# The output projection of the dilated layer, cut into chunks of 256 inputs and placed between the last four heads

## The reference

```
def second_block(x, c, ...):
    cond = silu(c)
    for i in range(2):
        mod = (cond @ ada_w[i] + ada_b[i]).reshape(B, 6, D)
        h = rms_norm(x, norm_mix[i]) * (1 + scale1) + shift1
        y = mla_mixer(h, ...) if i == 0 else dilated_mixer(h, ...)
        x = x + gate1 * y
        h = rms_norm(x, norm_mlp[i]) * (1 + scale2) + shift2
        x = x + gate2 * (square(relu(h @ mlp_w1[i])) @ mlp_w2[i])

def dilated_mixer(h, pos, w_in, g_q, g_k, rel_bias, w_o):
    # three groups of windows and dilations, 16 heads of 64; softmax over all of them
    ...
    return o.reshape(B, S, 1024) @ w_o
```

## Time and profile before

| | us |
|---|---|
| median of 3 runs | 1710.52 (1708.68 to 1711.46) |
| the profiled execution | 1711.83 |
| its span | 1709.9 |

### The profile page before, as it was taken

The page is one execution under the profiler, slowest core; times in us unless marked ns, Lnnn a source line. Parts: engine busy times, 40 slices in busy tenths (PEclk is TensorE's granted clock), DMA queues, the critical chain, the costliest instruction groups (busy, mean ns, idle before and its releaser), DMA issues.

```text
span 1709.9 us, 29065 instructions
## 1 busy us (share of the span) xinstructions
PE 1637.5 (96%) x12246; PEld 1544.7 (90%) x12246; DVE 1100.8 (64%) x1382; ACT 814.2 (48%) x1064; POOL 111.0 (6%) x99
## 2 busy tenths in 40 slices
PE   7999999999999999999888999989999999899998
PEld 6999989998999999999878899978999999889997
DVE  5768667775677668776685666667666555165554
ACT  5545443444545454444676544445444444254442
POOL 1040000000140000000020000001111110000000
PEclk9999999999999999999998999999999999599999
DMA  8765366666676456566432466666856454045552
GB/s 277 249 220 191 130 232 210 226 204 216 224 263 222 148 192 218 197 234 227 136 116 75 137 238 226 229 230 222 271 175 220 137 171 142 21 134 194 185 181 95
DMA packets 230242, 325.57 MB, mean 190 GB/s; under 512 B 7672, under 2 KB 199648, under 8 KB 229600
## 3 DMA queue, kind: packets, MB, share of 16 engines
q1 hardware_dynamic: 218696, 313.00, 54.5%
q10 hardware_dynamic: 11416, 10.71, 2.0%
HBM read 314.23 MB, written 9.45 MB: 189 GB/s over the span
## 4 chain that ended last, share of the span: by engine, by line
PE 75%; issue 9%; DVE 8%; ACT 4%; POOL 2%; DMA 1%; ACTq 0%; SPq 0%; DVEq 0%; POOLq 0%
PE bank L506 23%; PE bank L507 22%; PE bank L508 22%; PE bank L549 2%; DVE wlo L1496 2%; ACT whi L1044 2%; POOL rstd L983 2%; PE bank L570 1%; PE bank L874 1%; PE bank L702 1%; DVE ada_raw L1506 1%; PE bank L632 1%; DMA raw<-in_w_ffn_in 1%; PE bank L897 1%; DMA raw<-in_w_in 0%
## 5 line engine op out<-in xcount | busy, mean ns | idle before, releaser
L1496 DVE TENSOR_TENSOR wlo<-raw,whi 128x2048 fp32r<-128x2048 f32 (+1 forms) x241 | 550.5, 2287 | 282.2 <-ACT whi L1044 282.0
L1044 ACT ACTIVATE whi<-raw 128x2048 fp32r<-128x2048 f32 (+1 forms) x241 | 455.8, 1894 | 120.6 <-PE bank L508 96.9
L506 PE MATMUL bank<-hT_hi,whi 128*128 128x256 f32 x1728 | 495.6, 287 | 0.6 <-issue 0.3
L507 PE MATMUL bank<-hT_lo,whi 128*128 128x256 f32 x1728 | 490.3, 284 | 0.0
L508 PE MATMUL bank<-hT_hi,wlo 128*128 128x256 f32 x1728 | 490.1, 284 | 0.0
L506 PEld LDWEIGHTS bank<-hT_hi,whi 128*128 128x128 f32 x1728 | 332.6, 192 | 7.1 <-issue 5.5
L507 PEld LDWEIGHTS bank<-hT_lo,whi 128*128 128x128 f32 x1728 | 332.9, 193 | 1.2
L508 PEld LDWEIGHTS bank<-hT_hi,wlo 128*128 128x128 f32 x1728 | 332.8, 193 | 0.0
L506 PE MATMUL bank<-whi,hT_hi 128*128 128x256 f32 (+1 forms) x944 | 275.4, 292 | 4.1 <-DVE qn L1604 2.2
L507 PE MATMUL bank<-wlo,hT_hi 128*128 128x256 f32 (+1 forms) x944 | 270.4, 286 | 0.0
L508 PE MATMUL bank<-whi,hT_lo 128*128 128x256 f32 (+1 forms) x944 | 270.3, 286 | 0.0
(11 more groups left out here) (276 smaller groups left out, 1611.1 us busy)
## 6 DMA issues: line engine op xcount, KB each, us to landing
raw<-in_mlp_w SPq DMA_DIRECT2D x64, 1024.0 KB, 5.5
ada_raw<-in_ada_w SPq DMA_DIRECT2D x96, 512.0 KB, 6.2
raw<-in_w_in SPq DMA_DIRECT2D x44, 1024.0 KB, 5.4
raw<-in_w_ffn_in SPq DMA_DIRECT2D x44, 1024.0 KB, 5.3
raw<-in_dil_w_in SPq DMA_DIRECT2D x36, 1024.0 KB, 5.0
raw<-in_w_ffn_out SPq DMA_DIRECT2D x22, 1024.0 KB, 4.9
raw<-in_w_o SPq DMA_DIRECT2D x8, 1024.0 KB, 5.2
bias_near<-near SPq DMA_DIRECT2D x2, 3072.0 KB, 10.3
```

The lines of the kernel that those rows point to most:

```text
L506: pe.matmul(dst, lh, rh, start=start, stop=False)
L507: pe.matmul(dst, lh, rl, start=False, stop=False)
L1044: act.activation(view(whi[c % SPL], c), view(raw[c % RAW], c), ACT.Copy).then_inc(s_hi, 1)
L1496: dve.tensor_tensor(view(wlo[c % SPL], c), view(raw[c % RAW], c), view(whi[c % SPL], c).bitcast(F32), ALU.subtract).then_inc(s_lo, 1)
```

## The change

- The chunks of the dilated output projection are cut by inputs: chunk c holds 256 of the 1024 inputs and all 1024 outputs.
- The products are summed in four banks, one for each token half and output half, over all four chunks: 96 matmuls of 512 columns in 20 steps. `OUT_AT` places the steps between the parts of the last four heads; the last six stand behind the last pair.
- In the last group the scores, the transposes, the value products and the transposes of pairs use four fixed banks (`own`): first half of the scores and pairs the first, second half of the scores and the value products the second, the transposes the other two.
- The gate rows of this layer are made ahead of its first norm. VectorE multiplies them onto each raw chunk in place (`gate_weights`), ahead of the low part of the chunk before; ScalarE waits for that ahead of the high part.
- VectorE adds the four sums to `x` (`add_out`), without a multiplication. ScalarE squares 512 columns four times in the norm behind.
- The parts of chunk ("M1", 1, 1) are made behind that norm; before, they were made during the output projection.
- `wo()` remains for the first layer, unchanged.

```
-                    chunk(("MO", 1, c), kmajor(A["dil_w_o_2"][0], 256 * c, 256))
+                    chunk(("MO", 1, c), kmajor(A["dil_w_o_2"][0][256 * c:256 * c + 256, :], 0, D))
...
+        LAST = DH // HB - 1
+        OUT_AT = {("s", 0): (0, 1), ("s", 1): (2,), ("t", 1): (3, 4), ("s", 2): (5,), ("t", 2): (6, 7), ("s", 3): (8,),
+                  ("t", 3): (9,), ("t", 4): (10, 11), ("v", 4): (12, 13), ("o", 4): (14, 15, 16, 17, 18, 19)}
...
                     if i < HB:
                         ahead(j + 1)
+                        outward(j, "s", i)
                         exps(j, i)
                     if i:
                         turn_probs(j, i - 1)
                         ahead(j + 1)
+                        outward(j, "t", i)
                         values(j, i - 1)
+                outward(j, "v", HB)
                 ahead(j + 1, 3 * NG)
                 turn_pair(j, 1)
+                outward(j, "o", HB)
...
+            gate_rows(2, 16, 1)
             norm(6, xnd)
...
+                if (j, i) == (LAST, 0):
+                    own.extend([(n["w"] + k) % WB for k in range(WB)] + [(n["a"] + 4) % AB + WB])
...
+                    bk = begin("a", ("S", u, t), b=own_bank(j, t))
...
+                    bk = begin("a", ("T", u, t), b=own_bank(j, 2 + t))
...
+                bk = begin("w", ("O", u), b=own_bank(j, 1))
...
+            def project_out(step):          # TensorE
+                c, q = min(step // 4, 3), step % 4
+                ks = (0, 1) if c < 3 else ((step - 12) // 4,)
+                t, half = divmod(q, 2)
+                if step < 4:
+                    accs.append(begin("a", ("MO", 1, "sum", q)))
+                if q == 0:
+                    if c not in out_weights:
+                        out_weights[c] = weights(("MO", 1, c))
+                    for k in ks:
+                        emptied(pe, ("OT", unitd(2 * (2 * c + k)) // 2))
+                w = out_weights[c]
+                for k in ks:
+                    m = mm3(accs[q][:, :], aT_hi[:, 2 * c + k, P * t:P * t + P], aT_lo[:, 2 * c + k, P * t:P * t + P],
+                            w[0][:, k, 512 * half:512 * half + 512], w[1][:, k, 512 * half:512 * half + 512],
+                            (c, k) == (0, 0), (c, k) == (3, 1))
...
+            def project_out(step):          # ScalarE and VectorE
+                if step in (0, 4, 8):
+                    split_ahead(("MO", 1, step // 4))
...
+                    if c + 1 < len(chunks) and names[c + 1][:2] == ("MO", 1):
+                        gate_weights(c + 1)
                     dve.wait_ge(s_hi, c + 1)
...
+            def gate_weights(c):
+                emptied(dve, ("gb", 2, 1))
+                emptied(dve, ("gb", 2, 0))
+                dve.wait_ge(s_raw[c % RAW], 16 * (c // RAW + 1))
+                w = view(raw[c % RAW], c)
+                dve.tensor_tensor(w, w, gbc[:, :].unsqueeze(1).broadcast_to([P, 2, D]), ALU.mult).then_inc(s_scaled, 1)
+                dve.wait_ge(s_scaled, names[c][2] + 1)
...
+            def add_out():
+                for q in range(4):
+                    nm = ("MO", 1, "sum", q)
+                    t, half = divmod(q, 2)
+                    bk = full(dve, nm)
+                    xs = x[:, t, 512 * half:512 * half + 512]
+                    dve.tensor_tensor(xs, xs, bk[:, :], ALU.add).then_inc(drain_sem(nm), 1)
+                    emptied(dve, nm)
+                    dve.sem_inc(s_x2, 1)
```

More of the change, by code:

```diff
@@ L417, in forgetting_heads, with dilated @@
             last_gate(left.pop())
-        def dilated(project, scores, exps, turn_probs, values, turn_pair, ready):
+        LAST = DH // HB - 1
+        OUT_AT = {("s", 0): (0, 1), ("s", 1): (2,), ("t", 1): (3, 4), ("s", 2): (5,), ("t", 2): (6, 7), ("s", 3): (8,),
+                  ("t", 3): (9,), ("t", 4): (10, 11), ("v", 4): (12, 13), ("o", 4): (14, 15, 16, 17, 18, 19)}
+        def dilated(project, scores, exps, turn_probs, values, turn_pair, ready, project_out):
             left = [("D", j, g, m3) for j in range(DH // HB) for g, m3 in DIL_ORDER]
@@ L427, in ahead, with outward @@
                         project(left.pop(0))
+            def outward(j, *at):
+                if j == LAST:
+                    for n in OUT_AT.get(at, ()):
+                        project_out(n)
             ahead(0, 3 * NG)
@@ L474, in _, with begin @@
             freed, drains = {}, [0] * (WB + AB)
[L476 to L479, removed]
+            def begin(kind, name, freed_by=None, b=None):
+                if b is None:
+                    j, nb = n[kind], (WB if kind == "w" else AB)
+                    n[kind] += 1
+                    b = j % nb + (WB if kind == "a" else 0)
                 if b in freed:
@@ L543, in token_major, with turn @@
                 end(m, name)
[L545 to L546 removed]
+            def turn(name, src, nblk, w=P, kind="w", freed_by=None, b=None):
+                bk = begin(kind, name, freed_by, b)
                 for i in range(nblk):
@@ L848, in _, with own_bank @@
             latent_heads(queries, keys, turn_queries, turn_keys, begin_head, end_head, idle)
-            wo(0)
+            wo()
             mlp(0)
+            gate_rows(2, 16, 1)
             norm(6, xnd)
             todo = []
+            own, accs, out_weights = [], [], {}
+            def own_bank(j, i):
+                return own[i] if j == LAST else None
             def project(chunk_name):
@@ L881, in turn_probs @@
                 for t in range(TT):
-                    bk = begin("a", ("T", u, t))
-                    for n in range(4):
-                        m = pe.transpose(bk[:, P * n:P * n + P], Ld[u % 2][:, t, P * n:P * n + P], ident[:, :])
+                    bk = begin("a", ("T", u, t), b=own_bank(j, 2 + t))
+                    for k in range(4):
+                        m = pe.transpose(bk[:, P * k:P * k + P], Ld[u % 2][:, t, P * k:P * k + P], ident[:, :])
                     end(m, ("T", u, t))
@@ L893, in values @@
                         emptied(pe, ("D", j, g, 2))
-                bk = begin("w", ("O", u))
+                bk = begin("w", ("O", u), b=own_bank(j, 1))
                 for t in range(TT):
-                    for n, (g, kt) in enumerate(blocks(t)):
-                        m = pe.matmul(bk[:, HD * t:HD * t + HD], PTd[:, t, P * n:P * n + P],
-                                      Vd[j % 2][:, g, kt, HD * i:HD * i + HD], start=n == 0, stop=n == 3)
+                    for k, (g, kt) in enumerate(blocks(t)):
+                        m = pe.matmul(bk[:, HD * t:HD * t + HD], PTd[:, t, P * k:P * k + P],
+                                      Vd[j % 2][:, g, kt, HD * i:HD * i + HD], start=k == 0, stop=k == 3)
                 end(m, ("O", u))
@@ L904, in ready @@
                     emptied(pe, ("qkT", 8 + 6 * j + 2 * g + 1))
-            dilated(project, scores, idle, turn_probs, values, lambda j, p: turn_pair(unitd(HB * j + 2 * p) // 2), ready)
-            wo(1)
+            def project_out(step):
[14 more added lines that the diff above has]
+                            (c, k) == (0, 0), (c, k) == (3, 1))
+                if (c < 3 and q == 3) or step >= 16:
+                    n["acc"] += 1
+                    m.then_inc(s_acc, 1)
+                    chunk_done[chunk_at[("MO", 1, c)]] = (s_acc, n["acc"])
+                if step >= 16:
+                    nm = ("MO", 1, "sum", q)
+                    jobs[nm] = (s_acc, n["acc"]) + jobs[nm][2:]
+            dilated(project, scores, idle, turn_probs, values,
+                    lambda j, p: turn_pair(unitd(HB * j + 2 * p) // 2, own_bank(j, 0)), ready, project_out)
             mlp(1)
@@ L1040, in split_ahead @@
                     split_next[0] += 1
-                    act.wait_ge(s_raw[c % RAW], 16 * (c // RAW + 1))
+                    if names[c][:2] == ("MO", 1):
+                        act.wait_ge(s_scaled, names[c][2] + 1)
+                    else:
+                        act.wait_ge(s_raw[c % RAW], 16 * (c // RAW + 1))
                     if c >= SPL:
@@ L1053, in square @@
             def square(e, n, sq, t, part, a, b):
-                before = 4 * e + n - 1 + e % 2
+                before = 4 * e + n - 1 + (e in (1, 3, 5))
                 if before > 0:
@@ L2101, in values, with project_out @@
                 scale_out(unitd(HB * j + i))
+            def project_out(step):
+                if step in (0, 4, 8):
+                    split_ahead(("MO", 1, step // 4))
             dilated(project, scores, idle, idle, values,
-                    lambda j, p: at_low(unitd(HB * j + 2 * p) // 2, 2 * j + p, strided), idle)
-            wo(1)
+                    lambda j, p: at_low(unitd(HB * j + 2 * p) // 2, 2 * j + p, strided), idle, project_out)
+            add_out()
             mlp(1)
```

66 lines of the change are left out of this document (32 added, 34 removed).

## The result

The changed kernel takes 1689.6 us in the median of four executions (1688.3 to 1692.6), the kernel before 1710.6. The ratio is 0.9881, 95% interval [0.9864, 0.9898]: 20 us less by that ratio, 21.0 by the medians. The forecast was 1691.5 us. The profiled execution took 1690.6 us, its span is 1688.8.

What follows compares the result with a forecast made beforehand. TensorE idling or at lower clock, chiefly in the last four dilated heads, was taken as the bound. Stretch 21.8 less clock 2.6 and tail 0.2 gave 19.0 off 1711.8: 1692.8, with runs 1.3 lower 1691.5 us; range 1686 to 1702.

Steps and rivals of the forecast that it cites:

- The stretch: Last four dilated heads and output projection, first score to last projection matmul: 44.9 us instead of 66.7, before clock drops.
- 43 to 50 given as a sign: Expected microseconds from the last group's first score to the last projection matmul, with granted clock above 0.85.
- the walk: Step-by-step timing of TensorE, VectorE and ScalarE through the last four heads: waits of 4.5 us, stretch 44.9.
- Work: TensorE's work in the stretch after the change, at full clock: heads 18.6 us, projection 21.8, sum 40.4.
- Waits: TensorE in the stretch: 0.4 us in head 1, 2.0 in head 2's scores, 1.9 before values 2; 4.5 in all.
- Clock: Two waits of 2 us in the stretch cost one clock drop of 2.6 us, ends 0 and 6.8.
- half clock all the way: Rival: clock stays at half through the stretch, 75.8 us against 66.7, 9 slower, 1720; chance 0.04.
- Gate rows: They leave the stretch (3.62 us at half clock) for ahead of the dilated norm, where 1.9 us fit; cost 0.
- Before the stretch: VectorE's weight multiplications at 2.3 us each, those for chunks 0 to 2 before 1448; cost 0.
- Behind it: After the last projection matmul: mean square plus 0.2 us; second MLP chunk's split behind the norm costs 0, up to 0.3.
- No drop at all: Rival: the walk without any clock drop, 21.6 us less, 1689; chance 0.14.
- The chain of waits at every head: Rival: last four heads with four more waits of 1.5 us and two drops of 3.4, 1701.5 us; chance 0.22.

Runs made afterwards that it cites:

- the fillers: Against the changed kernel: all 20 steps behind the last pair, 78 matmuls of 512 columns with discarded sums between the heads; ratio 0.9963.
- the run with the later splits: Against the changed kernel: splits of the fourth output chunk and first MLP chunk made at steps 5 and 9 instead of 4 and 8; 1684.6 us, ratio 0.9857.
- the gate on the sums: Against the kernel with both splits at steps 5 and 9: gate multiplied onto the four sums instead of the weights; ratio 0.9863.
- the run with the split ahead: Against the kernel with splits at steps 5 and 9: second MLP chunk also split at step 14, ahead of the norm; ratio 0.9864.
- the other bank: Against the changed kernel: last group's value products share a bank with the second half of the transposes instead of the scores; ratio 0.9865.

## Why the prediction was right

**The stretch.** Forecast 66.7 - 21.8 + 2.6 = 47.5 us, measured 49.98, at the upper end of the 43 to 50 given as a sign. The mean clock was 0.90, above the 0.85 given, and the two waits stood where the walk had them. The mechanism was right: work in the place of waits and of half clock, shown by the fillers. Three sizes were off, and they partly cancel.
- Work. The sum of pieces was 40.4; it is 42.06. The pieces had been timed in runs of one kind, and most of the other 1.7 us lies in the joints between kinds. In the run with the later splits the first matmul of a group of steps is followed after 0.32 to 0.34 us and the next ones after 0.23 (1444.59, 1444.93, 1445.15), in ten groups: 1.0 us. This was not in the range of any term.
- Waits. 4.5 forecast, 2.6 measured. The two places and their causes were right, VectorE's low half of the fourth chunk ahead of the scaling, behind a shared bank, and ScalarE's high half ahead of the exponentials. They are 1.40 for 2.0 and 1.19 for 1.9, because TensorE itself arrived later than walked: it reached the first 15.0 us after the start instead of 14.7, and was released at 16.4 instead of 16.7. The wait of 0.4 us in head 1 is absent for the same reason: the values start at 12.05, with the copies done. The second was met 3.7 us later than walked and released 3.1 later, as it stands behind the first drop.
- Clock. I took one drop of 2.6 us; there are two, 3.4 and 1.7, of the sizes of the two rows whose mean I had taken. This is the term that was mis-sized most, by 2.5 us. The Trainium skill, "TensorE: Matmul & The Clock Gate", section "A second HAM failure mode: psum-queue depth-cycling", had warned of it: groups that cycle through banks leave short idles, and the clock falls and rises. The runs agree in part: here no banks are cycled, but two kinds of products share one, and with the value products moved to another the clock was 1.00. They don't agree with what I had made of it as a rival, half clock all the way.

**Outside the stretch.** The gain of 3.1 us ahead of the last group is no part of the change (the second profile of before has it too). It filled the place of the 2.5 us that the stretch was short, so 1692.8 forecast for the profiled execution met 1690.6. The forecast of the total is thus better than its parts, by luck. In the second comparison, on another chip, the changed kernel is 18.0 us shorter by the medians and 17.4 by the ratio, close to the 16.7 of the stretch and less than the 19.0 forecast.

**Gate rows.** They were forecast to leave the stretch with their time at half clock. Alone they give nothing, as they covered a wait; the forecast for the changed kernel held because steps stood there.

**Before the stretch.** The multiplications on the weights were taken at 2.3 us, beside other work. They take 2.28 each (L1558, four of them from 1424.9 to 1447.6), and with the gate on the sums the stretch is no shorter. This is shown for the later splits alone. In the changed kernel the multiplication at 1447.6 stands ahead of the chain that led to the first wait, as told above.

**Behind it.** The mean square was forecast 0.2 us later and comes 0.5 later (1496.68 - 1494.47 = 2.21 against 1.71), by the 0.83 us steps of the additions. (The 1514.93 that the prediction calls the last issue is the start of the gate rows behind it; both numbers are counted so, and the comparison holds.) The MLP split behind the norm was costed at 0; the trace of the run with the split ahead shows that it was a gain of 2.2 us at the mean square, which the times don't tell.

**Rivals.** No drop at all is what the later splits and the other bank gave, not the change. The chain of waits at every head didn't come: two waits of over 1 us. Half clock throughout didn't come either; its point of decision was 26 us of half clock and waits, the measured sum of lost time is 7.7.

## What to carry to other kernels

When a stage ends in many small dependent products, look at the granted clock of that window before counting idle time: here TensorE was busy for 37 of 44 us, at a clock of 0.57, and 17.7 us of dense work placed there were free. Then walk the lists of the other engines for the new places: two splits, each one position too early on VectorE and ScalarE, cost 7.9 us of the stretch in the profiles and 4 to 7 us of the time, mostly by the clock behind two short waits. Before removing an instruction from a slow stretch, ask which wait it covers.

## What the runs showed of the hardware that was not expected

- 78 matmuls of 512 columns, 17.7 us at full clock, added to 37.2 us of small products took 0.5 us there and gave 1.6 back behind them, through the clock.
- A wait of 1.22 us brought no drop of the clock where no drop had come before it; a wait of 1.19 at the same place brought 1.7 us of half clock in both profiles in which one of 1.4 us and its drop had gone ahead. What makes the difference is open.
- The twelve profiles reach the first transpose of the dilated layer's norm between 1149.8 and 1156.0 us, with the same list of instructions up to there but for the gate rows. The same kernel was there 2.7 us apart in the two profiles of before and 4.1 in the two of the changed kernel. A difference of that size outside the changed stretch says nothing of the change.
